# Expert units of 128 slots on the whole TensorE array, weights read in place from a ring of five

## The reference

```
g = argmax(xt @ w_rg + b_rg)                    # one of 4 groups
e_in = (xt @ w_re + b_re)[group g]              # 8 experts of that group
top_vals, top_idx = top_k(e_in, 2)              # two of them
h = silu(xt @ w_eg[e]) * (xt @ w_eu[e])         # 1024 -> 256, gate and up
y = y + weight * (h @ w_ed[e])                  # 256 -> 1024, down
```

## Time and profile before

| | us |
|---|---|
| three runs | 1369.9, 1370.3, 1374.34; median 1370.3 |
| profiled execution, its own time | 1369.2 |
| its span in the trace | 1367.5 |
| expert stage, first gate-up matmul to last down | 924.1 to 1309.5 |
| tail behind it | 1309.5 to 1367.5 |

### The profile page before, as it was taken

How to read it: one execution, slowest core, us unless ns; L and a number is a source line. 1 busy time by engine, 2 the same in 40 slices (tenths; PEclk the granted TensorE clock), 3 DMA queues, 4 the chain that set the end, 5 groups by cost and what they waited for, 6 DMA issues and landing times.

```text
span 1367.5 us, 23739 instructions
## 1 busy us (share of the span) xinstructions
PE 1162.8 (85%) x9144; PEld 657.2 (48%) x9145; DVE 703.9 (51%) x1252; ACT 326.6 (24%) x616; POOL 199.1 (15%) x278
## 2 busy tenths in 40 slices
PE   3999999999995999999798999747799997779820
PEld 3555555555554888889664555432233332223200
DVE  5178899842316788888532222461433423233246
ACT  5100011111112355555311111101222222222221
POOL 5000000000003222333000010011122222122000
PEclk8999999999997999999889999758999998999965
DMA  7311111110000011011333111454788887787356
GB/s 209 87 32 46 31 31 38 31 40 0 0 0 13 15 16 16 15 21 29 86 118 92 55 62 39 171 228 168 299 291 317 307 319 290 303 329 298 153 193 235
DMA packets 100795, 171.81 MB, mean 126 GB/s; under 512 B 47752, under 2 KB 72191, under 8 KB 91424
## 3 DMA queue, kind: packets, MB, share of 16 engines
q1 hardware_dynamic: 93215, 152.70, 32.5%
q0 software_dynamic: 7488, 17.84, 3.7%
HBM read 153.83 MB, written 26.11 MB: 132 GB/s over the span
## 4 chain that ended last, share of the span: by engine, by line
PE 71%; DVE 13%; issue 7%; DMA 4%; SPq 3%; ACT 2%; POOL 0%; DVEq 0%; POOLq 0%; ACTq 0%
PE ps L1416 25%; PE ps L1846 14%; PE ps L1720 9%; PE ps L1443 4%; PE ps L1876 3%; PE ps L1464 2%; DMA arena<-y_rows 1%; DVE arena L2150 1%; SPq L594 1%; DMA arena<-in_x_prompt_dram 1%; PE ps L1748 1%; PE ps L1452 1%; PE ps L1833 1%; DVE arena L2544 1%; DVE arena L2153 1%
## 5 line engine op out<-in xcount | busy, mean ns | idle before, releaser
L1416 PE MATMUL ps<-arena 128*128 128x512 f32 (+1 forms) x1056 | 346.3, 490 | 0.6 <-ACT arena L897 0.6
L1416 PEld LDWEIGHTS ps<-arena 128*128 128x128 f32 x1056 | 175.3, 192 | 172.8 <-issue 172.0
L1846 PE MATMUL ps<-arena 128*64 x416 | 203.3, 635 | 53.1 <-DVE arena L2544 52.2
L1849 PE MATMUL ps<-arena 128*64 128x512 f32 x416 | 203.4, 635 | 0.0
L1976 DVE SCALAR_TENSOR_TENSOR arena<-arena,cw 128x1024 f32<-128x1024 f32 x240 | 168.2, 778 | 0.4
L1846 PEld LDWEIGHTS ps<-arena 128*64 128x64 f32 x416 | 56.7, 145 | 177.2 <-issue 177.2
L1720 PE MATMUL ps<-arena 128*128 128x512 f32 (+1 forms) x288 | 128.8, 602 | 0.0
L2565 DVE COPY arena<-arena 128x4096 f32 x26 | 59.6, 2292 | 126.4 <-SPq L607 124.7
L1443 PE MATMUL ps<-arena 64*64 64x64 f32 x2864 | 98.7, 222 | 13.5 <-DVE arena L2162 9.9
L1443 PEld LDWEIGHTS ps<-arena 64*64 64x64 f32 x2864 | 91.9, 137 | 18.5 <-DVE arena L2162 11.0
L1876 PE MATMUL ps<-arena 128*64 x208 | 96.4, 606 | 2.4 <-ACT arena L1229 2.4
(11 more groups left out here) (323 smaller groups left out, 1513.2 us busy)
## 6 DMA issues: line engine op xcount, KB each, us to landing
arena<-in_w_exp_gate_dram SPq DMA_DIRECT2D x32, 1024.0 KB
arena<-in_w_exp_up_dram SPq DMA_DIRECT2D x32, 1024.0 KB
arena<-in_w_exp_down_dram SPq DMA_DIRECT2D x32, 1024.0 KB, 7.9
arena<-in_w_in_dram SPq DMA_DIRECT2D x22, 512.0 KB, 3.9
arena<-in_x_prompt_dram SPq DMA_DIRECT2D x16, 512.0 KB, 5.2
arena<-y_rows SPq DMA_DIRECT2D x8, 1024.0 KB
arena<-in_w_out_dram SPq DMA_DIRECT2D x2, 2048.0 KB, 9.7
xn_rows<-arena SPq DMA_DIRECT2D x8, 512.0 KB, 2.9
```

The lines of the kernel that those rows point to most:

```text
L1416: ins = pe.matmul(pr[:, n0:n1], win[q % 6][:, c, :], xnT[:, c, n0:n1], start=(c == 0), stop=(c == DC - 1))
L1846: pe.matmul(banks(b)[0:HS, :], xgT[b][:, c, 0:HS], wring_gu[:, bass.ds(slot, 1), 0:2, c, :].rearrange("p a w f -> p (a w) f"), start=(c == ...
L1849: ins = pe.matmul(banks(b)[HS:P, :], xgT[b][:, c, HS:P], wgu[b][:, :, c, :], start=(c == 0), stop=(c == DC - 1))
```

## The change

A unit is 128 slots of one expert. A unit is a group, and every matmul of the expert stage uses the whole 128 columns of the array (`banks(b)` instead of `banks(b)[0:HS]` and `banks(b)[HS:P]`). All weights are read from the ring by register; `wgu`, `wd`, `copy_gate_up`, `copy_down` and their waits go. The ring has five slots, the fifth where `xgT` and one `wgu` lay; it covers the routing's tables, so its first load waits for `rows_ready`. The first four loads go to the addresses of before. `gate_up` is issued in one piece, ahead of the transposes of hidden. PE itself now waits for the arrival of weights (`gu_here`, `wd_here`), with a second value taken from `unit_need` each time. `NUP` goes from 68 to 48.

```diff
-NQ = 2
-HS = P // NQ
-RW = 4
-NUNIT = NE + (N * TOPK - NE) // HS
-NUP = -(-NUNIT // (2 * NQ)) * 2 * NQ
-NGR = NUP // NQ
+RW = 5
+NUNIT = NE + (N * TOPK - NE) // P
+NUP = -(-NUNIT // 2) * 2
...
+def slot_of(e):
+    return (e + 1) % RW
...
             sp.wait_ge(turns_ready, 1)
...
-            for e in range(RW, NE + 3):
-                if e < NE:
+            expert = expert_at(AHEAD)
+            sp.wait_ge(rows_ready, 1)
+            for e in range(AHEAD, NE + 2):
+                if AHEAD < e < NE:
                     expert = expert_at(e)
                     sp.wait_ge(gu_psum, units_through(e - RW))
+                if e < NE:
                     load_gate_up(e, expert)
-                if e - 2 < NE:
-                    gate_up_arrived(e - 2)
-                if RW <= e - 1 < NE:
+                if e - 1 < NE:
+                    gate_up_arrived(e - 1)
+                if AHEAD <= e - 1 < NE:
                     expert = expert_at(e - 1)
-                    sp.wait_ge(yd_psum, units_through(e - 1 - RW))
+                    if e - 1 >= RW:
+                        sp.wait_ge(yd_psum, units_through(e - 1 - RW))
                     load_down(e - 1, expert)
-                down_arrived(e - 3)
+                down_arrived(e - 2)
...
-                if left >= 1:
-                    copy_down(g + 1, weights)
...
-            def slot_of(g):
-                return pe.value_load(unit_slot[0:1, bass.ds(NQ * g, 1)], min_val=0, max_val=RW - 1)
...
-                for c in chunks:
-                    pe.matmul(banks(b)[0:HS, :], xgT[b][:, c, 0:HS],
-                              wring_gu[:, bass.ds(slot, 1), 0:2, c, :].rearrange("p a w f -> p (a w) f"),
-                              start=(c == 0), stop=(c == DC - 1))
-                    ins = pe.matmul(banks(b)[HS:P, :], xgT[b][:, c, HS:P], wgu[b][:, :, c, :], start=(c == 0),
-                                    stop=(c == DC - 1))
...
+            def weights_of(g):
+                return (pe.value_load(unit_slot[0:1, bass.ds(g, 1)], min_val=0, max_val=RW - 1),
+                        pe.value_load(unit_need[0:1, bass.ds(g, 1)], min_val=1, max_val=NE))
+
+            def gate_up(g, b):
+                slot, need = weights_of(g)
+                pe.wait_ge(xT_act, 2 * NT + g + 1)
+                pe.wait_ge(xT_dve, 2 * NT + g + 1)
+                pe.wait_ge(gu_here, need)
+                for c in range(DC):
+                    ins = pe.matmul(banks(b), xgT[b][:, c, :],
+                                    wring_gu[:, bass.ds(slot, 1), 0:2, c, :].rearrange("p a w f -> p (a w) f"),
+                                    start=(c == 0), stop=(c == DC - 1))
+                ins.then_inc(gu_psum, 1)
...
+            def down(g):
+                slot, need = weights_of(g)
                 pe.wait_ge(ht_done, g + 1)
                 pe.wait_ge(ye_act, g)
                 pe.wait_ge(ye_dve, g)
-                pe.wait_ge(down_copied, g + 1)
+                pe.wait_ge(wd_here, need)
...
+            def pe_step(turn, b, left):
+
+                g = 2 * turn + b
+                if left >= 1:
+                    gate_up(g + 1, 1 - b)
+                transpose_hidden(g)
+                if left >= 2:
+                    transpose_rows(g + 2, turn + 1, b)
+                down(g)
...
             def dve_step(turn, b, left):
                 g = 2 * turn + b
-                if left >= 2:
-                    weights = weights_of(g + 2)
                 dve.wait_ge(ht_psum, g + 1)
                 dve.tensor_copy(hT.rearrange("p c n -> p (c n)"), banks(4)[:, 0:2 * P]).then_inc(ht_done, 1)
-                if left >= 2:
-                    copy_gate_up(g + 2, b, weights)
```

More of the change, by code:

```diff
@@ L64, with loads_in @@
 NCONV = 2 * CT
+def slot_of(e):
+    return (e + 1) % RW
+def loads_in(slot, through=NE):
+    return sum(1 for e in range(through) if slot_of(e) == slot)
 def rows_of(i):
@@ L270, in hybrid_decoder_step @@
         r_pid = take(1)
-        r_thr = take((NE - 1) // RW)
+        r_thr = take(NE // RW)
         r_rev, r_revs = take(1), take(NE)
@@ L279, in hybrid_decoder_step @@
         r_o = take(TOPK, NT, EG)
-        r_le, r_te, r_fl, r_fc = take(NE), take(1), take(1), take((NE - 1) // RW)
+        r_le, r_te, r_fl, r_fc = take(NE), take(1), take(1), take(NE // RW)
         r_col = take(2)
@@ L284, in hybrid_decoder_step @@
         r_key, r_order, r_low, r_high, r_pos, r_ncol, r_end, r_total = (take(1) for _ in range(8))
-        r_n, r_tn = take(1), take(NGR // 2)
+        r_n, r_tn = take(1), take(NUP // 2)
         O_OH = off[0]
@@ L309, in hybrid_decoder_step @@
         WSZ = 3 * DC * F
-        off[0] = O_ZS + NT * D
         xg = [late[:, s * D:(s + 1) * D] for s in range(2)]
         gain_f = xg[0]
-        xgT = [take(DC, P) for _ in range(2)]
         ye = [gain[:, :], small[:, 0:D]]
-        gs, gu = x_big[:, 0:F], x_big[:, F:2 * F]
-        wgu = [take(2, DC, F)]
-        O_W = off[0]
+        O_W = O_ZS + NT * D
         wring = at(O_W, RW, WSZ)
         wring_gu = at(O_W, RW, 3, DC, F)
-        assert O_W >= O_XN and O_W + RW * WSZ <= O_CO
+        assert O_RT >= O_W and O_W + WSZ >= O_XN and O_W + RW * WSZ <= O_CO
         off[0] = O_W + RW * WSZ
-        wgu.append(take(2, DC, F))
-        wd = take(2, D)
+        gs, gu = x_big[:, 0:F], x_big[:, F:2 * F]
         hT = take(2, P)
+        assert off[0] <= O_CO
+        off[0] = O_CO + D
+        xgT = [take(DC, P) for _ in range(2)]
+        assert off[0] <= O_EX
         g_idx = [sb(f"g_idx{s}", [P, 1], U32) for s in range(2)]
@@ L433, in hybrid_decoder_step @@
         rows_ready = sem("rows_ready")
-        wd_in = [w_loaded[5], *x_loaded]
-        wd_0 = [16 * len(range(5, MT, 6))] + [32 * (NT // 3)] * 3
-        gu_here, wd_here, gu_copied, down_copied = (sem(n) for n in ("gu_here", "wd_here", "gu_copied", "down_copied"))
+        wd_in = [w_loaded[5], *x_loaded, sem("wd_last")]
+        wd_0 = [16 * len(range(5, MT, 6))] + [32 * (NT // 3)] * 3 + [0]
+        gu_here, wd_here = sem("gu_here"), sem("wd_here")
         xg_zero = sem("xg_zero")
@@ L445, in hybrid_decoder_step @@
         yk_in = w_loaded[0:YS]
-        yk_0 = [wgu_0[s] + 32 * len(range(s, NE, RW)) for s in range(YS)]
+        yk_0 = [wgu_0[s] + 32 * loads_in(s) for s in range(YS)]
         ff_done, fin_done = sem("ff_done"), sem("fin_done")
@@ L617, in _ @@
             sp.wait_ge(h_done, NT)
-            for e in range(RW):
+            for e in range(AHEAD):
                 if e == 1:
                     sp.wait_ge(lg_psum, NT)
-                if e == RW - 1:
+                if e == AHEAD - 1:
                     sp.wait_ge(xn2_stored[0], 16 * ((NT + 1) // 2))
@@ L1218, in copy_xg @@
                     .then_inc(xT_act, 1)
[L1220 to L1231, removed]
             def act_step(turn, b, left):
@@ L1875, in pe_step @@
                         n0 = 2 * DC * F + c * D + half * 512
[L1876 to L1879 removed]
+                        ins = pe.matmul(banks(5 + half), hT[:, c, :],
+                                        wring[:, bass.ds(slot, 1), n0:n0 + 512].rearrange("p a n -> p (a n)"),
                                         start=(c == 0), stop=(c == 1))
[L1881 removed]
+                ins.then_inc(yd_psum, 1)
+            def pe_step(turn, b, left):
[6 more added lines that the diff above has]
+                down(g)
             transpose_rows(0, 0, 0)
             pe.wait_ge(turns_ready, 1)
[L1885 removed]
+            gate_up(0, 0)
             transpose_rows(1, 0, 1)
@@ L2448, in whole_units @@
             def whole_units(out, v, shift, scale=1.0):
-                TS(out, v, scale / HS, shift - 0.5 + 0.5 / HS, ALU.mult, ALU.add)
+                TS(out, v, scale / P, shift - 0.5 + 0.5 / P, ALU.mult, ALU.add)
                 TS(out, out, ROUND, None, ALU.add)
```

103 lines of the change are left out of this document (30 added, 73 removed).

## The result

The changed kernel takes 1427.35 us (median of 4 runs, 1422.73 to 1429.36) against 1370.1 us before: a ratio of 1.0413, with 95% interval 1.037 to 1.0456. The profiled execution took 1429.36 us with a span of 1427.6 us. I had forecast slower, 1438 us, in 1428 to 1453.

A forecast was written before the change was run, and what follows sets the result against it. It took the expert stage as four fifths PE work, one fifth weight supply through copies. Twelve more groups at 11.8 us (+142 us), less 73 us of waits and slow clock, gave 1438 us, 68 us slower; range 1428 to 1453.

The forecast's parts named there:

- Rival 3: Expert-stage matmuls: halves of a pair took turns, a single record costs half; kernel ends near 1305 us; chance 0.02.
- Rival 2: Weight supply still bounds single-unit stretches: at 291 GB/s a unit takes 12.5 us, kernel 1457 us; chance 0.09.
- my 345 GB/s: DMA rate in one window before, at share 0.90; taken to show the needed 308 GB/s is possible.
- Rival 1: PE's register loads not covered at each gate-up: 33 us, kernel 1471 us, or 1455 for half; chance 0.07.
- Rival 4: Expert-loop padding: only 32 units, so 30 full steps and 1367 us, no change; chance 0.02.
- I take 11.8 us for a step, with 11.6 and 12.0 as ends: PE time of one expert-stage group after the change, against 12.00 us before; 36 full steps make 424.8 us.
- the 0.11 us: Output projection: edge of 32 full-tile records over 32 steps, taken as an edge without a switch of tile.
- my edge of 0.15 us: Expert-stage group before: what a piece of PE work costs over its 0.43 us steps.
- 11.45 us: Expert-stage step if each of four tile switches cost its whole 0.15 us edge; sum 13 us lower; not adopted.
- The start: Before the expert loop: routing -2.0 us, first gather +1.5 us, first gate-up at 923.6, loop from 938.0 us.
- 9.25 + 3.7 + 1.5: First to second gate-up: gate-up 9.25 us, table load through products and row copy 3.7, half clock 1.5.
- The 73 us: Expert stage beyond 312 us of PE work, read as weight supply through copies; nearly all to be given back.

The follow-up runs named there:

- experiment 3: Changed kernel with its five-slot weight ring refilled as if it had four slots; 1425.89 us, ratio 1.0411 to the kernel before.
- experiment 7: Changed kernel's frame with 26 groups of two 64-slot units, no weight copies, ring refilled as four slots, second half's result left out; 1296.71 us, ratio 0.9456.
- experiment 4: Changed kernel with the hidden transposes put back into the middle of the gate-up, all matmuls still full-array; one run, 1429.35 us.
- experiment 5: Changed kernel with hidden transposes mid-gate-up and each full record split into two half tiles, second half's result left out; one run, 1443.27 us.
- experiment 6: Changed kernel's frame with 26 groups of two 64-slot units, no weight copies, ring of five, second half's result left out; 1298.24 us, ratio 0.9493.
- experiment 10: Experiment 9's kernel with the gate-up issued in one piece, two changes of tile shape a step instead of four; 1304.24 us, ratio 0.952.
- experiment 9: Experiment 8's kernel with DVE doing products and the copy of rows ahead of the copy of gate-up weights; 1308.48 us, ratio 0.9558.
- experiment 1: Changed kernel run again with no edit, for spread and the early part; 1427.01 us, ratio 1.0418.
- experiment 8: Kernel before, with only SP's words of weight arrival given one round earlier; 1307.58 us, ratio 0.9538.
- experiment 11: Experiment 7's kernel with SP's words of weight arrival given one round later, as in the kernel before; 1320.98 us, ratio 0.9642.

## Why the prediction was nearly right and the range too high

**The main terms held.** The trace has 38 groups, a full-array record steps by 0.43 us, and 12 groups more outweigh the stalls that go. Rival 3 (a half record costs half) is out by that step. Rival 2 (supply) is out by experiments 3 and 7: my 345 GB/s was only what had been asked for, the DMA gives 423. Rival 1 (register loads) is out: two loads stand between a down and the next gate-up, and from the down's start to that gate-up it is 953.81 - 950.36 = 3.45 us, which is its 8 records. Rival 4 is out by the 38 groups.

**The step that failed is the size of a step, "I take 11.8 us for a step, with 11.6 and 12.0 as ends"; it measured 11.41.** 36 steps times 0.39 are 14.0 us, and 11.41 lies below my lower end of 11.6. I had taken the 0.11 us by which 32 full-tile records of the output projection exceed 32 steps for an edge that every piece has, and left only 0.05 us for the four changes of shape. Experiments 4 to 7, and 10 against 9, show the opposite: a piece has no edge and a change of shape costs 0.15 us. Half of that cost I had never looked for: my edge of 0.15 us was read on the half-tile records alone, and as much again lay inside the transposes, 0.15 us in the two of hidden and 0.15 in the eight of rows (see the result), which I had booked as their own time. The Trainium skill (TensorEngine Tiling (Array Packing), Key Properties) says that a change of mode drains TensorE; by that I had worked out 11.45 us and a sum 13 us lower, and set it aside. The runs agree with the page. That my 11.45 comes so near is in part chance, since its 0.4 us is not four times 0.15; 12.00 - 4 x 0.15 is 11.40. The 0.11 us of the projection has another place: of its 32 records the first takes 0.68 us and the later ones 0.59, in steps of 0.43, and ahead of the first stand 16 matmuls with 36 moving columns. Why a record is longer behind those stays open.

**The start, term by term**, against the traces. The part ahead came 3.2 us later in the profiled execution (experiment 1). The routing gave back 0.6 us instead of 2.0 (from the last projection tile to the gather 62.4 against 63.0 us): its 36 records with 48 columns take 8.41 us, with 68 columns 8.54, so the columns weren't their price. The gather took 7.49 us where I had 5.1. From the first gate-up to the second it was 942.30 - 930.66 = 11.64 us where I had 9.25 + 3.7 + 1.5 = 14.45: the sigmoid's table was loaded while PE worked (ACT had nothing else to do any more), and after a pause of only 1.28 us the granted clock was still 1.00 (2.4 GHz). Together 3.2 + 1.4 + 2.4 - 2.8 = 4.2 us later than forecast. The end of the stage, 16.4 us for my 15.9, and the tail, 58.1 for 58.0, were right. The sum: 1436.7 + 4.2 - 14.0 + 0.5 + 0.1 = 1427.5, and the span is 1427.6. By the step alone the time would have been 1424; in this execution the later start hid some of it, 3.2 us of which are scatter, and its own 1429.36 us lie inside the range. That the median came within 1 us of the range is in part luck.

**The 73 us were given back as forecast, but my reading of them was wrong.** I called them supply of weights. They came from SP's word of arrival, given behind waits for PE (experiments 8, 11), with DVE's copy, products and rows behind it. This did not move the forecast, since the change removes the whole chain, but it hid that the word moved by one round gives back 62 us by itself: the changed kernel pays 12 more groups, 137 us, to get rid of waits that needed none of them.

## What to carry to other kernels

With 512 moving columns, a matmul with 64 stationary columns costs as much as one with 128, and a unit with few rows as much as a full one, so count units, not slots, before you drop a packing of two tiles. When an engine waits for an in-order queue's word that data is there, read what stood ahead of the word in that queue: in the kernel before, the data had arrived and the word stood behind a wait for the very engine that was waiting. And group the matmuls of one tile shape together, since each change of shape is paid, and read what it costs on both sides of the change.

## What the runs showed of the hardware

A change between 128x64 and 128x128 tiles costs 0.15 us on TensorE at full clock (11.40, 11.69 and 12.00 us a step with zero, two and four of them in experiments 4, 7 and 5), for float32 matmuls of 512 columns and transposes.

The DMA engines moved 423 GB/s at a share of 1.02, while TensorE read weights without a wait (experiment 7).

POOL's indirect DMA takes longer while DVE copies weights from SBUF to SBUF. Groups by line of 930 to 1300, POOL's gathers: count, busy us, mean ns, idle time ahead; the kernel before:

```profile
L850 POOL DMA_INDIRECT late<-xn_rows,g_idx x23 | 40.3, 1750 | 19.6 <-POOL g_idx L847 19.6
```

experiment 7, which has no such copy:

```profile
L862 POOL DMA_INDIRECT late<-xn_rows,g_idx x24 | 24.9, 1037 | 20.4 <-POOL g_idx L859 20.4
```

and experiment 9, where the copy falls on the gather in nearly every step:

```profile
L852 POOL DMA_INDIRECT late<-xn_rows,g_idx x23 | 60.9, 2649 | 19.6 <-POOL g_idx L849 19.6
```

Such a gather takes 1,037 ns on the mean without the copy and 2,649 ns (median 2,818) in experiment 9, while the copy's own 2.28 us do not change. The Trainium skill (SBUF — State Buffer, SBUF: two separate sides) says that such a copy in float32 keeps GpSimd from writing its descriptors; the rows agree. Here POOL had the time to spare, and nothing waited for it.
